# Two fused model blocks on one core: an expert ring of eleven buffers, logits by token, and an earlier scatter of the last but one expert

## The reference

```python
hn = rms_norm_2(h, w_norm_ffn)
aff = softmax(einsum('btd,de->bte', hn, w_router))          # 16 experts
top_aff, top_idx = top_k(swapaxes(aff, 1, 2), cap)          # cap = 2 * 272 // 16 = 34 tokens for each expert
xg = hn[bi, top_idx]
hg = einsum('becd,edf->becf', xg, w_gate)                   # 1024 -> 2048
hu = einsum('becd,edf->becf', xg, w_up)
y = einsum('becf,efd->becd', silu(hg) * hu, w_down)         # 2048 -> 1024
h = h + zeros_like(hn).at[bi, top_idx].add(y * top_aff[..., None])
return rms_norm_2(h[:, 16:], w_norm_final)
```

## Time and profile before

| | us |
|---|---|
| median of 3 runs | 1977.05 |
| lowest and highest | 1975.39, 1980.61 |
| profiled execution | 1974.44 |
| its span in the trace | 1972.7 |
| TensorE busy | 1793.3 |
| VectorE busy | 685.2 |
| ScalarE busy | 593.4 |

### The profile page before, as it was taken

The page is one execution under the profiler, slowest core; times in us unless marked ns, Lnnn a source line. Parts: engine busy times, 40 slices in busy tenths (PEclk is TensorE's granted clock), DMA queues, the critical chain, the costliest instruction groups (busy, mean ns, idle before and its releaser), DMA issues.

```text
span 1972.7 us, 20940 instructions
## 1 busy us (share of the span) xinstructions
PE 1793.3 (91%) x8339; PEld 1047.7 (53%) x8339; DVE 685.2 (35%) x1304; ACT 593.4 (30%) x1037; POOL 19.6 (1%) x50
## 2 busy tenths in 40 slices
PE   8878789999899999779989998999988899998887
PEld 6767678888787877558762232223322222232222
DVE  0366236650458999842122111111111111111111
ACT  1142312220254734553013332212232222332222
POOL 3000000000000000000000000000000000000000
PEclk9889899999999999889999998989899998999998
DMA  4320124444334434213957999999999999999995
GB/s 166 107 86 1 38 102 157 150 152 149 120 139 152 173 117 143 86 64 110 381 202 302 428 427 428 427 427 427 428 427 428 426 428 427 427 428 426 429 426 251
DMA packets 43790, 523.29 MB, mean 265 GB/s; under 512 B 4856, under 2 KB 5048, under 8 KB 5944
## 3 DMA queue, kind: packets, MB, share of 16 engines
q1 hardware_dynamic: 42336, 511.23, 63.5%
q10 hardware_dynamic: 1368, 10.85, 1.6%
HBM read 520.95 MB, written 1.12 MB: 265 GB/s over the span
## 4 chain that ended last, share of the span: by engine, by line
PE 75%; DVE 13%; issue 5%; ACT 3%; DVEq 3%; DMA 0%; ACTq 0%
PE psum L1003 24%; PE psum L978 12%; PE psum L506 11%; PE psum L764 6%; DVE arena L1777 4%; PE psum L739 4%; PE psum L986 3%; PE psum L849 3%; DVE arena L1765 2%; PE psum L721 2%; PE psum L942 1%; DVEq L1779 1%; PE psum L540 1%; PE psum L531 1%; PE psum L967 1%
## 5 line engine op out<-in xcount | busy, mean ns | idle before, releaser
L1003 PE MATMUL psum<-arena 128*34 128x512 f32 x2048 | 477.1, 619 | 77.9 <-issue 77.3
L1003 PEld LDWEIGHTS psum<-arena 128*34 128x34 f32 x2048 | 142.2, 115 | 387.2 <-issue 386.4
L764 PE MATMUL psum<-arena 128*128 128x272 f32 x1408 | 329.5, 393 | 11.7 <-DVE arena L1947 10.0
L764 PEld LDWEIGHTS psum<-arena 128*128 128x128 f32 x1408 | 266.8, 190 | 70.0 <-DVE arena L1947 10.4
L1477 DVE SCALAR_TENSOR_TENSOR arena<-psum,arena 34x512 f32<-34x512 f32 x64 | 43.8, 684 | 710.1 <-ACT arena L1074 710.1
L506 PE MATMUL psum<-arena 128*128 128x256 f32 x1120 | 246.3, 382 | 5.1 <-DVE arena L1492 4.0
L978 PE MATMUL psum<-arena 128*34 128x512 f32 x1024 | 247.3, 639 | 0.5 <-ACT arena L1451 0.5
L506 PEld LDWEIGHTS psum<-arena 128*128 128x128 f32 x1120 | 213.1, 191 | 37.6 <-issue 6.2
L978 PEld LDWEIGHTS psum<-arena 128*34 128x34 f32 x1024 | 61.5, 119 | 173.2 <-issue 172.0
L1440 ACT ACTIVATE arena<-psum 34x512 f32<-34x512 f32 x64 | 38.2, 597 | 358.2 <-PE psum L1003 358.2
L1777 DVE SCALAR_TENSOR_TENSOR arena<-arena 128x272 f32<-128x272 f32 x240 | 105.3, 499 | 4.4 <-issue 0.4
(11 more groups left out here) (378 smaller groups left out, 1445.3 us busy)
## 6 DMA issues: line engine op xcount, KB each, us to landing
arena<-in_experts SPq DMA_DIRECT2D x192, 2048.0 KB, 33.9
arena<-in_panels SPq DMA_DIRECT2D x91, 1024.0 KB, 4.8
arena<-in_down_panels SPq DMA_DIRECT2D x8, 1408.0 KB, 6.0
arena<-scr ACTq DMA_DIRECT2D x4, 2176.0 KB, 9.0
out<-arena SPq DMA_DIRECT2D x2, 512.0 KB, 2.7
arena<-in_x_cols SPq DMA_DIRECT2D x1, 544.0 KB, 4.7
arena<-in_x_cols ACTq DMA_DIRECT2D x1, 544.0 KB, 5.2
arena<-in_w_norm_final ACTq DMA_DIRECT2D x1, 512.0 KB, 7.0
```

Source lines behind the costliest of these rows:

```text
L764: ins = mm(pair[k][:, b, 0:T], slot8[k][:, c, b * P:(b + 1) * P], src[:, c, :], start=c == 0, stop=c == DC - 1)
L1003: ins = mm(psum[64 * x:64 * x + CAP, p % 2, :], xg[:, c, :], r_up[t % RING][:, c, :], start=c == 0, stop=c == DC - 1)
```

## The change

The ring gets eleven slots instead of nine. To make room, small tiles are laid out anew: the constants that live to the end (`ident`, `esmall`, `slots_iota`, and a copy `ffn2_s` of one parameter) go to the very front, so that all the stretch behind them (`low`) can hold two ring slots once the logits are done; `es`, `up_row`, `h_row` use partitions 0 to 33 and 64 to 97 of the same columns in turn, `xt` and `ysb` share columns, `otT` moves. The first panels are issued in another order: 4 and 5 behind i = 7, 6 behind g = 1, 7 behind g = 2, 8 after the last `w_out_2` panel, 9 and 10 after the logits. The load of `wfin` moves from ScalarE's queue in the router to the end of SP's.

The logits are computed as tokens x experts at once. The top choice reads the affinities in PSUM. The first gather finishes half 0 first, and ScalarE and VectorE copy one half each. `scatter(14)` runs after pair 1 of expert 15. The last `ysb` is copied by ScalarE and VectorE, half each, and the final scaling and the stores go by halves (four DMAs).

The diff, cut to its core:

```diff
-RING = 9
+RING = 11
...
-        ident, m_gt, m_lt = cut(P), cut(P), cut(P)
+        ident, esmall, slots_iota, ffn2_s = cut(P), cut(64), cut(CAP), cut(DC)
+        low = top[0]
+        m_gt, m_lt = cut(P), cut(P)
...
-        ring = [cut(4096) for _ in range(3)]
-        es, up_row = cut(2, 512), cut(2, 512)
+        ring = [cut(4096) for _ in range(4)]
+        es, up_row = cut(512), cut(512)
...
-        ring.append(arena[:, base_dense:base_dense + 4096])
+        ring.append(arena[:, low + 4096:low + 8192])
+        ring.append(arena[:, low:low + 4096])
+        wfin, squared = ring[5][:, 0:D], ring[6][:, 0:D]
...
+        xt = cut(2 * 512)
+        ysb = xt[64:64 + CAP, :]
+        ones_r = cut(T)
...
-        h_row = cut(4, 512)
+        h_row = cut(2, 512)
@@ sync
                 if i == 7:
+                    expert_panel(0, 4)
                     sp.wait_ge(ev("gsig_ready"), after["gsig_ready"] + 2)
-                    expert_panel(0, 4)
+                    expert_panel(0, 5)
             for g in range(4):
                 panel(PANELS["w_out_2"] + g)
                 if g == 1:
-                    expert_panel(0, 5)
+                    expert_panel(0, 6)
                 if g == 2:
                     sp.wait_ge(ev("merged_ready"), after["merged_ready"] + 4)
-                    expert_panel(0, 6)
+                    expert_panel(0, 7)
             for last in (n[0] - 2, n[0] - 1):
                 sp.wait_ge(panel_done[last % 2], last // 2 + 1)
-            for t in range(7, 12 * E):
+            expert_panel(0, 8)
+            sp.wait_ge(ev("lg_done"), after["lg_done"] + 1)
+            for t in range(9, 12 * E):
...
-            for tb in range(2):
-                sp.wait_ge(ev("out_ready"), tb + 1)
-                sp.dma_start(out[0][tb * P:(tb + 1) * P, :], h_tok[:, tb, :]).then_inc(ev("stored"), 16)
-            sp.wait_ge(ev("stored"), 32)
+            sp.wait_ge(ring_done[5], (12 * E - 1) // RING)
+            sp.dma_start(wfin, a["w_norm_final_2"].rearrange("(a n) -> a n", a=1).to_broadcast([P, D])).then_inc(ev("wfin_loaded"), 16)
+            for i in range(4):
+                tb, half = i // 2, slice(512 * (i % 2), 512 * (i % 2) + 512)
+                sp.wait_ge(ev("out_ready"), i + 1)
+                sp.dma_start(out[0][tb * P:(tb + 1) * P, half], h_tok[:, tb, half]).then_inc(ev("stored"), 16)
+            sp.wait_ge(ev("stored"), 64)
@@ tensor
-            def logits(first, last):
-
-                pe.wait_ge(ev("hsq_ready"), last // 2)
-                for c in range(first, last):
-                    mm(ms_bank[0:META, 0:1], sqm[:, c, :], ones[:, 0:1], start=c == 0, stop=c == DC - 1)
-                for c in range(first, last):
-                    ins = mm(lgT_bank[0:E, 0:T], w_r[:, c, :], hT[:, c, :], start=c == 0, stop=c == DC - 1)
+            def logits(i):
+
+                for c in range(2 * i, 2 * i + 2):
+                    for ck in (1, 2, 0):
+                        t0, nt = TOK[ck]
+                        ins = mm(lg_bank[0:nt, ck * E:(ck + 1) * E], hT[:, c, t0:t0 + nt], w_r[:, c, :],
+                                 start=c == 0 and ck == 1, stop=c == DC - 1, skip_group_check=True)
                 return ins
...
-            logits(0, 6)
+            logits(0)
             turn_part(3)
-            logits(6, DC).then_inc(ev("lgT_done"), 1)
-            pe.wait_ge(ev("lgT_copied"), after["lgT_copied"] + 1)
-            for ck, (t0, nt) in enumerate(TOK):
-                ins = nc.tensor.transpose(lg_bank[0:nt, ck * E:(ck + 1) * E], left[0:E, t0:t0 + nt], ident[0:E, 0:E])
-            ins.then_inc(ev("lg_done"), 1)
+            pe.wait_ge(ev("hsq_ready"), 4)
+            for c in range(DC):
+                ins = mm(ms_bank[0:META, 0:1], sqm[:, c, :], ones[:, 0:1], start=c == 0, stop=c == DC - 1)
+            ins.then_inc(ev("lgT_done"), 1)
+            for i in range(1, 3):
+                logits(i)
+            logits(3).then_inc(ev("lg_done"), 1)
...
+            pe.wait_ge(ring_loaded[0], 16)
             for _ in range(7):
-                mm(psum[:, 1, :], ident, par[:, 0:512], start=True, stop=True)
+                mm(psum[:, 1, :], ident, ring[0][:, 0:512], start=True, stop=True)
...
+            def first_gather():
+
+                pe.wait_ge(ev("oh_ready"), after["oh_ready"] + 1)
+                for half in range(2):
+                    for tb in range(2):
+                        ins = mm(psum[64 * half:64 * half + CAP, 2, :], ohg[:, tb, :],
+                                 h_tok[:, tb, half * 512:(half + 1) * 512], start=tb == 0, stop=tb == 1)
+                    ins.then_inc(ev("gathered_half" if half == 0 else "gathered"), 1)
+                pe.wait_ge(ev("xt_half"), after["xt_half"] + 1)
...
-            gather(0)
+            first_gather()
...
-                            ins = mm(psum[64 * x:64 * x + CAP, p % 2, :], xg[:, c, :],
+                            lo = 64 * (x ^ (p % 2))
+                            ins = mm(psum[lo:lo + CAP, p % 2, :], xg[:, c, :],
                                      r_up[t % RING][:, c, :], start=c == 0, stop=c == DC - 1)
...
+                    if p == 1 and e + 1 == E:
+                        scatter(e - 1)
...
-                if e:
+                if e and e + 1 < E:
                     scatter(e - 1)
@@ scalar
-            act.dma_start(wfin, a["w_norm_final_2"].rearrange("(a n) -> a n", a=1).to_broadcast([P, D])).then_inc(ev("wfin_loaded"), 16)
...
-            copy_gathered(0)
+            act.wait_ge(ev("gathered_half"), after["gathered_half"] + 1)
+            A(xt[0:CAP, 0:512], psum[0:CAP, 2, :], ACT.Copy).then_inc(ev("xt_copied"), 1)
...
-                for half in range(2):
-                    A(ysb[0:CAP, half * 512:(half + 1) * 512], psum[64 * half:64 * half + CAP, 2, :], ACT.Copy)
+                for half in range(2 if e + 1 < E else 1):
+                    A(ysb[:, half * 512:(half + 1) * 512], psum[64 * half:64 * half + CAP, 2, :], ACT.Copy)
@@ vector
-            CP(left[0:E, :], lgT_bank[0:E, 0:T]).then_inc(ev("lgT_copied"), 1)
...
-            CP(affT[0:E, :], psum[0:E, 0, 0:T])
-            CP(left[0:E, :], psum[0:E, 0, 0:T])
-            dve.drain()
+            affT = psum[0:E, 0, 0:T]
...
-            v.memset(affT[0:E, :], 1.0)
-            dve.drain()
-            v.tensor_tensor_scan(pos[0:E, :], affT[0:E, :], left[0:E, :], 0.0, MUL, ADD)
+            v.tensor_tensor_scan(pos[0:E, :], ones_r[0:E, :], left[0:E, :], 0.0, MUL, ADD)
...
+            dve.wait_ge(ev("gathered"), after["gathered"] + 1)
+            CP(xt[0:CAP, 512:1024], psum[64:64 + CAP, 2, :]).then_inc(ev("xt_half"), 1)
...
+            dve.wait_ge(ring_done[(12 * E - 1) % RING], (12 * E - 1) // RING + 1)
+            CP(ysb[:, 512:1024], psum[64:64 + CAP, 2, :]).then_inc(ev("ex_half"), 1)
```

More of the change, by code:

```diff
@@ L289, in two_blocks @@
         sqm = cut(DC, META)
-        xt, xg = cut(2 * 512), cut(DC, CAP)
-        ysb = cut(D)
+        xg = cut(DC, CAP)
         ring.append(arena[:, upper - 4096:upper])
@@ L298, in two_blocks @@
         ring.append(arena[:, mark1:mark1 + 4096])
-        ring.append(arena[:, base_dense:base_dense + 4096])
+        ring.append(arena[:, low + 4096:low + 8192])
+        ring.append(arena[:, low:low + 4096])
+        wfin, squared = ring[5][:, 0:D], ring[6][:, 0:D]
+        top[0] = mark1 - 512 - 2 * DC * T + 4096
+        otT = [cut(S) for _ in range(2)]
+        assert top[0] <= mark1
         top[0] = mark1 + 8192
         h_tok = cut(2, D)
-        wfin = cut(D)
+        xt = cut(2 * 512)
+        ysb = xt[64:64 + CAP, :]
+        ones_r = cut(T)
         assert top[0] <= upper - 8192
-        top[0] = base_dense + 4096
-        affT, left, pos = cut(T), cut(T), cut(T)
-        assert top[0] <= base_dense + 2 * 11 * PW
-        h_row = cut(4, 512)
+        top[0] = low + 8192
+        left, pos = cut(T), cut(T)
+        top[0] = low + 8192
+        h_row = cut(2, 512)
         hx = cut(EB, CAP)
@@ L983, in scatter @@
                 pe.wait_ge(ev("ex_out"), after["ex_out"] + e + 1)
+                if e == E - 1:
+                    pe.wait_ge(ev("ex_half"), after["ex_half"] + 1)
                 for tb in range(2):
                     for half in range(2):
[L986 to L987 removed]
+                        ins = mm(psum[:, 4 + 2 * tb + half, :], otT[e % 2][64:64 + CAP, tb * P:(tb + 1) * P],
+                                 ysb[:, half * 512:(half + 1) * 512], start=False, stop=e == E - 1, skip_group_check=True)
                     if e == E - 1:
@@ L1066, in copy_panels, with sigmoid_ln @@
                     n[0] += 1
[L1068 removed]
+            def sigmoid_ln(tmp, x, name, one=None):
                 A(tmp, x, ACT.Abs)
@@ L1477, in sigmoid_arg @@
                 STT(tmp, x, 0.0, tmp, ALU.min, SUB).then_inc(ev(name + "_arg"), 1)
+            v.memset(one_col, 1.0)
             v.memset(eps_t, EPS).then_inc(ev("eps_ready"), 1)
@@ L1974, in _ @@
             v.memset(ss, 0.0)
```

(14 more changed lines are left out.)

60 lines of the change are left out of this document (29 added, 31 removed).

## The result

The changed kernel takes 1960.91 us (median of 4 runs, 1960.08 to 1961.44), the kernel before 1978.19 in the same comparison (1975.39 to 1980.61): ratio 0.9923, 95% interval 0.9907 to 0.994. It is 17.3 us faster by the medians, and 14.4 by the two profiled spans (1972.7 and 1958.3). The forecast was 1964, range 1957 to 1970.

What follows compares the result with a forecast made beforehand. Bound: the expert weight stream, 4.91 us a panel. First release +2.35, two slots -9.8 and tail -4.4 gave -11.9 us: 1962.5 from the profiled execution, 1965.2 from the median; said 1964, range 1957 to 1970.

Steps and rivals of the forecast that it cites:

- The bound and the two slots: Expert stage: the weight stream at 427 GB/s bounds it; two more panels fill its standstill, saving 9.8 us.
- The third rival: Ring: the two slots gain nothing, as panels 9 and 10 come too late or TensorE bounds; 1973.8 us, chance 0.05.
- The early load: Expert panel 5 ahead of the first `w_out_2` panel: 2.8 us more stand plus 1.7 of slow clock, cost 4.5 us.
- The first rival: Early load costs nothing, as the queue interleaves or TensorE does not stand; 1959.5 us, chance 0.2.
- The first release: First ring slot freed at the end of expert 0's first pair: 2.35 us later, bounds -2.3 and +6.
- The logits: Router: logits by token, small matmuls replacing wide ones, copy and transposes; 1.1 us saved (0.2 to 2.3).
- The top choice: Router: two copies (0.85 us) and a memset (0.4) go, up to 0.3 lost, taken as 0.2.
- The gather: First gather: copies side by side, but only the middle matmuls overlap; gain 0.9 or loss 2.0 us, taken as 0.
- The tail: Expert 15 to the end: earlier scatter 3.6, split copy 0.4, halved output 0.4; -4.4 us (bounds -3 and -6).
- The second rival: Small costs go badly: slow gather, logits at 4.8 us, slow first pairs, poor tail; up to 1969.8 us, chance 0.16.
- The fourth rival: Expert pairs: exchanged halves lose matmul overlap, a pair nearing 13.6 us, some 2300 us in all; chance 0.02.

Runs made afterwards that it cites:

- pairs by side: Changed kernel with each pair's eight matmuls to one half of the output partitions all before the eight to the other: 2208.89 us, one run.

## Why the prediction was right, and where not

**The bound and the two slots: right.** The stream ran at 427 GB/s, and from first release to the end every kernel with eleven filled slots, the early scatter and the new tail took 908.75 to 909.6 us, whether the release came at 1044.3 or at 1052.8 (pairs by side aside, where TensorE is the bound). Emptying two slots cost 9.8 us, the forecast's 9.8. The gain is the standstill that is filled, not the depth. The third rival, that the slots do nothing, is out.

**The early load: right,** 4.64 us against 4.5, by its two parts: 3.0 us more stand (said 2.8) and 1.65 at half clock (said 1.7). That this is the cause was shown once panel 5 was moved and the 4.6 us came back. The first rival, that it costs nothing, is out.

**The first release** came 1.55 us later from the first mark (70.21 and 68.66), where the forecast said 2.35. The misses of its terms largely cancel. Its recorded lower bound, -2.3, is not the sum of its own terms, which give -4.4 (0, 2.3, 0.85, 0.4, and 0.9 for the gather); nothing hangs on it.

**The logits: wrong,** in sign. The step that failed is "32 such entries and 16 short ones are 4.8 us", meant as the upper end. At full clock 12 entries took 1.36 us, a rate at which the 36 others would take 4.1: 5.4 together, 0.6 more than 4.8 (an estimate from that row). I had priced the 16-column loads of L909 for the narrow token block, and let the other entries be no dearer than those of the turn. The rest is the clock, which I hadn't priced at all: it fell to half under work that never paused. In the best executions it fell for the last 2 us (4.92, so 6.3 together), and with the early load sooner, up to 1.2 us more. Together +1.68 where I said -1.1.

**The top choice: right,** -1.08 against -1.05.

**The gather: wrong,** in mechanism and size. The step that failed is "In the new order only the middle ones alternate: 7 steps of 0.43 us instead of 4.5", which lets two matmuls in a row on one half lose their overlap. They don't: the eight entries took 1.92 us, and half 0 is ready no earlier than half 1 (the copies start at 1040.24 and 1040.30), so that the new order gains nothing. The gain of 2.0 us is 1.5 by the clock (3.45 and 1.92, the same eight entries) and 0.5 by the two copies side by side. In twelve of thirteen profiled executions with changes the gather ran at 1.92, where the seven fillings, or others in their place, end close to it; the one with a bare stand of 1.01 us before the turn of `pos` was slow, as was the kernel before with 0.92. So most of it seems to be the kernel's and not chance, though only one profile of the kernel before says so. The first pair's -1.69, though, was luck: in all six other executions with the early load, pairs by side left aside, it took 8.77 or more.

**The tail: right, somewhat low.** 15.44 - 9.8 = 5.6 against 4.4. By the traces, `down(15, 1)` ended 912.7 us after the first release in the kernel before and 898.5 after, 4.4 less besides the 9.8 (said 3.6), and from there to the end it took 10.3 instead of 11.6, 1.3 less (said 0.8). Of the 1.3, 0.4 is the last scatter, 3.67 instead of 4.08 us, which is the clock. Of the 4.4, by the undone edit, about 2 is the scatter at full clock; most of the rest is pair 3, 7.08 instead of 8.77 us, which the forecast had counted. The single undoings gave 5.5 (scatter) and 2.0 (copy, scaling, stores), both with a slow stretch of the clock; without it about 2 and 1.1.

**The sum.** The misses were +2.8 (logits), -2.0 (gather), -1.7 (first pair), -1.2 (tail) and -0.5 (code that did not change), which makes -2.5 to -2.6: 14.4 instead of 11.9. So the number is closer than its terms, since a miss of 2.8 one way hides half of 5.4 the other way. The second rival had the logits too cheap still, and its slow gather, slow first pair and poor tail did not come. The other 3 us of the 17.3 are no effect: the profiled execution of before was 3.75 below its median, that of after 0.83.

**The fourth rival** had the right mechanism for another order: losing the overlap makes TensorE the bound and costs hundreds of us, but exchanging the sides in every second pair does not lose it.

## What to carry to other kernels

When a stage is bound by a stream, count the panels that are there when it restarts: two filled slots were worth exactly two panels, and neither an earlier release nor the mere depth of the ring changed the rate. A prefetch ahead of a transfer that somebody waits for, on the same full queue, is not free; one panel too early cost 4.6 us here, and moving it by one place gave that back. A price read from one instance can be an exception: the scatter of expert 15 was one of three out of 15 without a slow stretch behind it. Cut the trace at marks and compare stretches, since unchanged code moved the whole time by up to 6 us between executions.

## What the runs showed of the hardware that I had not expected

- The granted clock fell to 0.50 (1.2 of 2.4 GHz) while TensorE was busy in every window: in the logits, on entries that moved 16 columns (with 64 it stayed at 1.00 there, in one profile), and around the scatter, on entries of 512 columns (0.50 from 1946 to 1948 with the scatter put back). A stand is not needed for it, and the forecast counted on a stand alone.
- Matmuls to the lower and the upper half of the output partitions overlapped even when two of a side came in a row: 7.10 us for 16 of 512 columns in blocks of two, 7.08 alternating, 12.06 in blocks of eight (the first and last from one run each). The 1.6 us saved there out of 13.65 are about four entries of 0.43; that TensorE works about that far ahead fits this and is not shown by itself.
- One more 2 MB transfer ahead on a full queue moved a landing from 7.0 to 12.0 us after issue, by about the 4.91 us that such a panel takes. By the Trainium skill, page "DMA: Bandwidth & Descriptors", section "Queues, rings and completion order", descriptors are consumed in ring order on each engine; the two landings agree.
